# Layer 2 of a two-block model on one core: the first gate tile projected inside the query and key projections

## The chip, the core and the metric

The kernel runs on one core of one Trainium2 chip. The metric is the device time of one execution in microseconds, of which a run gives one number; lower is better. The span in the profile is the time from the first to the last instruction of the program on the core, and is a little shorter than the device time. TensorE's clock has two levels here, 2.4 GHz (written 1.00 in the rows) and 1.2 GHz (0.50).

## What is computed

Two blocks of two layers each work on 512 tokens of 1024 features in float32. The first block has a mixer of dilated windows (layer 1) and a differential attention (layer 2); the second has twice a hybrid mixer and a feed-forward part. Only layer 2 is touched. Its core is this:

```
def diff_mixer(h, w_in, lq1, lk1, lq2, lk2, subln, w_out, lambda_init):
    proj = h @ w_in
    q = proj[..., :DIFF_QK_WIDTH]
    k = proj[..., DIFF_QK_WIDTH:2 * DIFF_QK_WIDTH]
    v = proj[..., 2 * DIFF_QK_WIDTH:2 * DIFF_QK_WIDTH + DIFF_WIDTH]
    gate = proj[..., 2 * DIFF_QK_WIDTH + DIFF_WIDTH:]
    ...
    p = jax.nn.softmax(s, axis=-1)
    a = p[:, 0] - lam * p[:, 1]
    ...
    o = rmsnorm(o, subln) * (1.0 - lambda_init)
    y = o.reshape(B, S, DIFF_WIDTH) * jax.nn.silu(gate)
    return y @ w_out
```

There are 8 heads of 128 value columns; each head has two softmaxes over causal scores.

## The kernel before

**One list of steps, five queues.** The class `Order` writes one list of steps for the whole program, and each engine (TensorE, VectorE, ScalarE, GpSimd, and SyncE for the DMAs) then walks that list and issues its own part of each step. So the list is also the order on every engine, and an engine waits in place for whatever its next instruction needs. Every product of float32 is made as three: weights and activations are held as a high part and a rest, and high times high, high times rest and rest times high are added up.

**Weights.** `weight_tiles` lists the weight tiles in the order in which they are used. A tile is split into its two parts when its turn comes (step `split`, the high part by ScalarE at L2161 or L2165; steps `lo`, the rest by GpSimd at L3151 or L3153), into one of three places that are used in turn.

**Main and side.** In layer 2 (`layer2`) a main generator issues projections in pieces: `wide` for the values (tiles l2v0 and l2v1, L1789), `rotated` for queries and keys (l2q0 to l2q3 and l2k0 to l2k3, pieces of 12 matmuls at L1782; each tile is followed by its rotary step on VectorE, L2527: `rope` reads the banks, `rotate` combines, and the DMAs of `spread` lay the result out), and `gates` for the gate tiles (l2g0 to l2g3, pieces of 12 matmuls of 256 columns, L1789). `beside` lets the side generator, the attention, advance by a fixed ratio for each piece: R_L2 = 1.2 beside the projections and R_G2 = 1.35 beside the gates.

**Attention.** There are 32 units, 8 for each pair of heads (p = 0 to 3); a unit is one head and one block of 128 queries, with 128 to 512 keys. The blocks of the eight units of a pair have 128, 384, 256, 256, 128, 384, 512 and 512 keys, in this order (`L2_ORDER`). A unit n goes through five stages, of which several units are in flight: `scores2` (TensorE L1955 into banks 4 and 5; then VectorE masks and reduces, L2774), `exp2` (ScalarE L2321), `mix2` (VectorE L2786 to L2791), `turn2` (TensorE transposes the weights, L1966; ScalarE copies them, L2346), `out2` (TensorE L1977; ScalarE squares and scales the sums, L2335 and L2337). Scores need both banks 4 and 5, so the next scores wait for VectorE to have reduced the ones before. The transposes, the sums and the transposes of the gated output (`chunk`, TensorE L1855, ScalarE L2206, VectorE L2573) share two corner banks, 6 and 7, which are taken in turn: each user waits until the last but one has been read out.

**Waits of the main generator.** The queries of pair 2 are held back until the attention of pair 0 is through (`while p >= 2 and p - 2 not in attended`), and gate tile j until pair j is normalized (`done(j)`; `square2` on VectorE, a power on GpSimd at L3168, `norm2` on VectorE). While the main generator is held back, only attention steps are issued, and TensorE has no projection to do between them. A gate tile j is projected, `gate` makes gate times (1 + tanh) in `fat(3072..)` (ScalarE L2291, VectorE L2686), `times` multiplies the normalized output by it (VectorE L2700), and `chunk` transposes it for the output projection.

## Time and profile before

| | us |
|---|---|
| Median of 3 runs | 2664.75 (2664.47 to 2665.68) |
| The profiled execution, device time | 2664.24 |
| The profiled execution, span | 2662.9 |
| TensorE busy with matmuls | 2616.2 (98%) |
| VectorE busy | 1227.3 (46%) |
| ScalarE busy | 1039.0 (39%) |
| GpSimd busy | 1141.6 (43%) |

The busy times are averages over stages that differ. Matmuls overlap, and their recorded ends are modelled; where a stretch is costed closely, the distance from one start to the next is the better measure. An idle time is printed behind the row of the instruction that it precedes, with what ended it.

### The profile page before, as it was taken

To read this page: it belongs to the slowest core of one execution; us is meant where nothing else is said; L and a number is where in the kernel's file an instruction comes from. 1 tells how busy PE (TensorE), PEld (TensorE's weight loads), DVE (VectorE), ACT (ScalarE), POOL (GpSimd) and SP (SyncE) were. 2 spreads that over 40 slices of the span, in tenths; PEclk is the share of its full clock that TensorE was granted. 3 is DMA by queue.
4 is the path that set the end of the run, shared out by engine and by line. 5 is a ranking of instruction groups with operands and counts; after the bars stand their busy time and mean duration, and the time that the engine had idled before them with its cause. 6 is when DMAs were issued, how large, how long until landed. Compare 5 with 4: busy or idle time off the path is not lost.

```text
span 2662.9 us, 35461 instructions
## 1 busy us (share of the span) xinstructions
PE 2616.2 (98%) x13561; PEld 2122.7 (80%) x13561; DVE 1227.3 (46%) x2446; ACT 1039.0 (39%) x1937; POOL 1141.6 (43%) x894
## 2 busy tenths in 40 slices
PE   8999999989999999999999999999999999999998
PEld 6887878768778877777888888887777788888887
DVE  3535344543565456445245424265544524642426
ACT  4343434443446344452333424234435333342422
POOL 4434434435442443333464444444333336544443
PEclk9999999999999999999999999999999999999999
DMA  6434333332331332224352333324222435233331
GB/s 195 129 105 120 103 110 112 112 111 85 114 92 60 110 102 80 80 83 143 107 175 80 111 95 99 99 77 136 86 73 91 135 107 183 72 118 95 95 95 64
DMA packets 215053, 282.15 MB, mean 106 GB/s; under 512 B 21982, under 2 KB 155586, under 8 KB 214116
## 3 DMA queue, kind: packets, MB, share of 16 engines
q1 hardware_dynamic: 214884, 279.88, 34.1%
q8 instruction: 108, 1.77, 0.3%
q14 instruction: 61, 0.50, 0.1%
HBM read 246.21 MB, written 16.84 MB: 99 GB/s over the span
## 4 chain that ended last, share of the span: by engine, by line
PE 93%; DVE 3%; ACT 2%; POOL 1%; issue 1%; DMA 0%; DVEq 0%; ACTq 0%; POOLq 0%
PE banks L1789 36%; PE banks L1786 31%; PE banks L1782 13%; PE banks L1807 2%; PE banks L1921 1%; PE banks L1903 1%; PE banks L1846 1%; PE banks L1955 1%; PE banks L2022 1%; PE banks L2049 1%; PE banks L1977 1%; PE banks L1889 1%; PE banks L2035 1%; DVE AR L2527 1%; PE banks L2100 1%
## 5 line engine op out<-in xcount | busy, mean ns | idle before, releaser
L3153 POOL TENSOR_TENSOR WS<-WR,WS 128x512 fp32r<-128x512 f32 (+2 forms) x676 | 856.9, 1301 | 1030.1 <-ACT WS L2165 1030.1
L1789 PE MATMUL banks<-WS,UT 128*128 128x512 f32 (+1 forms) x3312 | 720.6, 370 | 4.8 <-DVE UT L2527 4.8
L1786 PE MATMUL banks<-UT,WS 128*128 128x512 f32 (+1 forms) x3024 | 705.1, 392 | 0.7 <-ACT AR L2354 0.7
L1786 PEld LDWEIGHTS banks<-UT,WS 128*128 128x128 f32 (+1 forms) x3024 | 561.8, 187 | 129.3 <-issue 12.0
L1789 PEld LDWEIGHTS banks<-WS,UT 128*128 128x128 f32 x3312 | 559.8, 188 | 116.2 <-issue 18.1
L2165 ACT ACTIVATE WS<-WR 128x1024 fp32r<-128x1024 f32 (+1 forms) x344 | 333.2, 1018 | 215.7 <-PE banks L1789 139.0
L1782 PE MATMUL banks<-UT,WS 128*128 128x512 f32 x1536 | 365.8, 394 | 0.0
L1782 PEld LDWEIGHTS banks<-UT,WS 128*128 128x128 f32 x1536 | 283.9, 188 | 63.7 <-issue 5.9
L1789 PE MATMUL banks<-WS,AT 128*128 128x512 f32 x1296 | 300.7, 390 | 3.8 <-POOL WS L3153 3.3
L1789 PEld LDWEIGHTS banks<-WS,AT 128*128 128x128 f32 x1296 | 242.7, 188 | 55.1 <-POOL WS L3153 3.7
L3151 POOL TENSOR_TENSOR WS<-WR,WS 128x512 fp32r<-128x512 f32 x128 | 179.6, 1434 | 231.1 <-ACT WS L2161 231.1
L2527 DVE TENSOR_TENSOR AF<-banks,AF 128x512 f32<-128x512 f32 x128 | 94.0, 786 | 188.9 <-PE banks L1782 188.7
L3088 DVE SCALAR_TENSOR_TENSOR AR<-banks,AR 128x511 f32<-128x511 f32 x84 | 63.0, 750 | 211.7 <-ACT AR L2496 211.7
L3168 POOL TENSOR_TENSOR SM<-SM 128x1 f32<-128x1 f32 (+2 forms) x44 | 47.4, 1076 | 238.0 <-DVE SM L3056 90.9
L2527 DVE TENSOR_TENSOR AR<-AR,banks 128x512 f32<-128x512 f32 x80 | 57.4, 724 | 169.2 <-PE banks L1789 157.5
L2527 DVE TENSOR_TENSOR AR<-AR 128x512 f32<-128x512 f32 (+3 forms) x93 | 93.3, 1003 | 16.3 <-ACT AR L2246 12.9
L2496 ACT ACTIVATE AR<-banks,AR 128x512 f32<-128x512 f32 x84 | 65.1, 774 | 89.4 <-PE banks L1786 79.7
L2161 ACT ACTIVATE WS<-WR 128x512 fp32r<-128x512 f32 x128 | 69.9, 622 | 57.4 <-PE banks L1782 57.4
L2629 DVE CUSTOM_DVE_ANT_0 AF<-banks,MF 128x256 f32<-128x256 f32 (+1 forms) x128 | 44.4, 402 | 101.7 <-PE banks L1889 86.4
L2527 DVE TENSOR_TENSOR AF<-AF 128x512 f32<-128x512 f32 x64 | 88.7, 1424 | 0.7
L1786 PE MATMUL banks<-AT,WS 128*128 128x512 f32 x384 | 87.4, 389 | 0.0
L1786 PEld LDWEIGHTS banks<-AT,WS 128*128 128x128 f32 x384 | 72.1, 188 | 15.0
(224 smaller groups left out, 2517.0 us busy)
## 6 DMA issues: line engine op xcount, KB each, us to landing
WR<-in_w_in SPq DMA_DIRECT2D x112, 512.0 KB, 3.6
WR<-in_w_up SPq DMA_DIRECT2D x88, 512.0 KB, 3.5
WR<-in_dil_w_in SPq DMA_DIRECT2D x64, 512.0 KB, 3.7
WR<-in_w_down SPq DMA_DIRECT2D x40, 512.0 KB, 3.7
WR<-in_diff_w_in SPq DMA_DIRECT2D x32, 512.0 KB, 3.8
WR<-in_dil_w_in SPq DMA_DIRECT2D x32, 256.0 KB, 3.7
AR<-AF SPq DMA_DIRECT2D x128, 64.0 KB, 2.7
AR<-AF SPq DMA_DIRECT2D x64, 128.0 KB, 2.6
```

Of the source, the lines that this page charges most:

```text
L1782: mm = pe.matmul(B[bank][:, :], slot(i, part)[:, c:c + P], act[:, other, kk, :], start=start, stop=stop)
L1786: mm = pe.matmul(B[bank][0:c, :], w[part][:, kk, g * P:g * P + c], act[:, other, kk, :], start=start, stop=stop)
L1789: mm = pe.matmul(B[bank][:, off:off + n], act[:, other, before_k + kk, g * P:g * P + P], w[part][:, kk, :], start=start, stop=stop)
L1807: mm = pe.matmul(B[c][:, 256 * half:256 * half + 256], w[x][:, kk, (c % 2) * P:(c % 2) * P + P], UT[:, y, kk, 256 * half:256 * half + 256] ...
L2161: x = se.activation(slot(i, 0)[:, to].rearrange("p (a f c) -> p a f c", f=2, c=32), src, ACT.Copy)
L2165: se.activation(slot(i, 0)[:, v * h:v * h + h], raw(i)[:, v * h:v * h + h], ACT.Copy).then_inc(hi.sem, 1)
L2496: se.activation(d, B[order.bank[i, half][0]][:, :], ACT.Identity, scale=cp[:, 2, f:f + 1], bias=cp[:, 3, f:f + 1]).then_inc(conv_id.sem, 1)
L2527: return ve.tensor_tensor(out_, x, y, op)
L3088: ve.scalar_tensor_tensor(d[:, 1:T], bank[:, 0:T - 1], cp[:, 1, f:f + 1], d[:, 1:T], ALU.mult, ALU.add).then_inc(dve_step, 1)
L3151: ge.tensor_tensor(low, src, high.bitcast(F32), ALU.subtract).then_inc(lo_p.sem, 1)
L3153: ge.tensor_tensor(slot(i, 1)[:, s], raw(i)[:, s], slot(i, 0)[:, s].bitcast(F32), ALU.subtract).then_inc(lo_p.sem, 1)
L3168: ge.tensor_tensor(SM[:, o:o + n], SM[:, o:o + n], SM[:, MHALF:MHALF + n], ALU.pow).then_inc(rstd.sem, 1)
```

## The change

The first gate tile, l2g0, moves in the list of tiles and in the list of steps: it is projected right after the second tile of values, ahead of the queries of pair 2. Its `gate` step (ScalarE and VectorE) goes with it. Its `times` steps stay with the gates: `gates` now begins with them, once pair 0 is normalized, and then goes on with tile l2g1. The last hunk of the diff keeps a wait pointing at the gate tile before, now that it is not the neighbour in the list.

```
--- before.py
+++ after.py
@@ -118,9 +118,11 @@
     for p in range(4):
         if p % 2 == 0:
             wide(f"l2v{p // 2}", w, 2048 + 256 * p)
+        if p == 2:
+            out.append(("l2g0", KC, 256, [(0, cols(w, 3072))]))
         for name, o in (("q", 0), ("k", 1024)):
             out.append((f"l2{name}{p}", KC, 256, [(0, cols(w, o + 256 * p))]))
-    for j in range(4):
+    for j in range(1, 4):
         out.append((f"l2g{j}", KC, 256, [(0, cols(w, 3072 + 256 * j))]))
     joined("l2o", ap["diff_w_out"][0])
     for l in range(2):
@@ -519,9 +521,15 @@
             self.hybrid(l)
             self.ffn(l)
 
-    def gates(self, name, done, late, gated):
+    def gates(self, name, done, late, gated, early=()):
+        for i, half, j in early:
+            while not done(j):
+                self.tick()
+                yield 1
+            self.step("times", i, half, j)
+            self.soon(4 + 2 * half, lambda half=half: self.step("chunk", name, half))
         across = self.feature_major if name == "l1g" else self.token_major
-        for j in range(4):
+        for j in range(1 if early else 0, 4):
             while j < 3 and not done(j):
                 self.tick()
                 yield 1
@@ -646,11 +654,16 @@
         self.step("natural_table")
 
     def layer2(self):
-        projected, attended, normed = set(), set(), set()
+        projected, attended, normed, early = set(), set(), set(), []
 
         def project(p):
             if p % 2 == 0:
                 yield from self.wide(f"l2v{p // 2}", self.plain("copy", "2v", p), fresh=(p == 0))
+            if p == 2:
+                def deal(i, half):
+                    self.step("gate", i, half, 0)
+                    early.append((i, half, 0))
+                yield from self.token_major("l2g0", deal)
             while p >= 2 and p - 2 not in attended:
                 yield 1
             for name in "qk":
@@ -701,7 +714,7 @@
         late = []
         att = attention()
         self.beside(main(), att, R_L2)
-        self.beside(self.gates("l2g", lambda j: j in normed, late, set()), att, R_G2)
+        self.beside(self.gates("l2g", lambda j: j in normed, late, set(), early), att, R_G2)
         self.lower(self.splits)
         self.drain(att)
         self.flush()
@@ -2287,7 +2300,7 @@
                     i, half, j = a
                     se.wait_ge(proj.sem, proj.at[i, half if tiles[i][0][:3] == "l1g" else 2 * half + 1])
                     if j > 0:
-                        se.wait_ge(timed.sem, timed.at[i - 1, half])
+                        se.wait_ge(timed.sem, timed.at[index[f"{tiles[i][0][:3]}{j - 1}"], half])
                     se.activation(fat(3072 + 512 * half, 512), B[gate_bank(i, half)][:, :], ACT.Tanh,
                                   scale=0.5).then_inc(tanhed.sem, 1)
```

No instruction is added or removed but the grouping; what changes is the place of each. In the rows below a name before `<-` is what is written, those behind it what is read; WS holds split weights, UT the layer's input, CT the identity, AF, AR and MF are work space. Rows of the attention's scores (L1955) and sums (L1977) have twice the count in the trace; projections and transposes stand one for one. Line numbers from L1782 on are 13 higher in the changed kernel.

**TensorE, from the last piece of l2g1 to the first piece of l2g2, before:**

```order
L1789 MATMUL banks<-WS,UT 128x256 x12
L1966 MATMUL banks<-CT,MF 128x128 x4
L1955 MATMUL banks<-AR 128x256 x4
L1977 MATMUL banks<-AR,AF 128x128 x4
L1966 MATMUL banks<-CT,AF 128x128
L1855 MATMUL banks<-CT,AR 128x128 x4
L1977 MATMUL banks<-AR,AF 128x128
L1966 MATMUL banks<-CT,AF 128x128 x3
L1855 MATMUL banks<-CT,AR 128x128 x4
L1955 MATMUL banks<-AR 128x128 x2
L1955 MATMUL banks<-AR 128x384 x2
L1789 MATMUL banks<-WS,UT 128x256 x12
```

**The same place now,** the first 12 rows from the last piece of l2g1 on:

```order
L1802 MATMUL banks<-WS,UT 128x256 x12
L1968 MATMUL banks<-AR 128x512 x2
L1990 MATMUL banks<-AR,AF 128x128 x2
L1979 MATMUL banks<-CT,MF 128x128
L1968 MATMUL banks<-AR 128x512 x2
L1868 MATMUL banks<-CT,AR 128x128 x4
L1990 MATMUL banks<-AR,AF 128x128
L1979 MATMUL banks<-CT,AF 128x128 x3
L1968 MATMUL banks<-AR 128x128 x2
L1968 MATMUL banks<-AR 128x384 x2
L1868 MATMUL banks<-CT,AR 128x128 x4
L1990 MATMUL banks<-AR,AF 128x128 x3
```

Before, the last 12 matmuls of l2g1 stood behind the sums of unit 22, and 10 rows of attention separated them from l2g2 (the last row). Now they stand ahead of the scores of unit 22 (the first row of 512). All 11 rows shown behind them are attention and `chunk`; 10 more follow, from the transposes of unit 22 to the scores of units 28 and 29, before the first 12 matmuls of l2g2.

**VectorE, after the rotary products of the last key tile (l2k3), before:**

```order
L2786 RECIPROCAL SM<-SM 128x2
L2788 SCALAR_TENSOR_TENSOR SM<-SM 128x1
L2791 SCALAR_TENSOR_TENSOR MF<-MF,SM 128x384
L2527 TENSOR_TENSOR AF<-AF 128x512 x2
L2774 ISA AF,SM<-banks,CT 128x256
L2774 ISA SM 128x1
L2774 ISA AF,SM<-banks,CT 128x256
L2774 ISA SM 128x1
```

**The same place now:**

```order
L2799 RECIPROCAL SM<-SM 128x2
L2801 SCALAR_TENSOR_TENSOR SM<-SM 128x1
L2804 SCALAR_TENSOR_TENSOR MF<-MF,SM 128x384
L2713 SCALAR_TENSOR_TENSOR AR<-AF,AR 128x2x256 x2
L2540 TENSOR_TENSOR AF<-AF 128x512 x2
L2787 ISA AF,SM<-banks,CT 128x256
L2787 ISA SM 128x1
L2787 ISA AF,SM<-banks,CT 128x256
L2787 ISA SM 128x1
```

The two `times` instructions of l2g0 (AR<-AF,AR) now stand between the mix of unit 17 (the row MF<-MF,SM) and the rotation of l2k3 (AF<-AF 128x512 x2). The reduction of unit 19 stands behind them.

**TensorE, the end of pair 1's attention, before:**

```order
L1977 MATMUL banks<-AR,AF 128x128
L1782 MATMUL banks<-UT,WS 128x512 x12
L1966 MATMUL banks<-CT,AF 128x128 x3
L1977 MATMUL banks<-AR,AF 128x128 x3
L1966 MATMUL banks<-CT,MF 128x128 x4
L1977 MATMUL banks<-AR,AF 128x128 x4
L1782 MATMUL banks<-UT,WS 128x512 x12
L1966 MATMUL banks<-CT,AF 128x128 x4
L1977 MATMUL banks<-AR,AF 128x128 x4
L1782 MATMUL banks<-UT,WS 128x512 x60
```

**The same place now:**

```order
L1990 MATMUL banks<-AR,AF 128x128
L1979 MATMUL banks<-CT,AF 128x128 x3
L1795 MATMUL banks<-UT,WS 128x512 x12
L1990 MATMUL banks<-AR,AF 128x128 x3
L1979 MATMUL banks<-CT,MF 128x128 x4
L1990 MATMUL banks<-AR,AF 128x128 x4
L1979 MATMUL banks<-CT,AF 128x128 x4
L1990 MATMUL banks<-AR,AF 128x128 x4
L1795 MATMUL banks<-UT,WS 128x512 x96
```

Before, one piece of the key tile stood between the sums of unit 14 and the transposes of unit 15. Now units 13, 14 and 15 end in one stretch with no piece between them.

## Rows read from the trace of the kernel before

**Rows 1.** From the page: engines' busy time; the chain that ended last.

```profile
PE 2616.2 (98%) x13561; PEld 2122.7 (80%) x13561; DVE 1227.3 (46%) x2446; ACT 1039.0 (39%) x1937; POOL 1141.6 (43%) x894
...
PE 93%; DVE 3%; ACT 2%; POOL 1%; issue 1%; DMA 0%; DVEq 0%; ACTq 0%; POOLq 0%
```

**Rows 2.** Timeline of TensorE, hole before l2g2: start, us, what, [idle before it].

```profile
824.99 1.66 PE L1789 MATMUL banks<-WS,UT 128*128 128x256 f32 x12
...
832.76 0.88 PE L1966 MATMUL banks<-CT,AF 128*128 128x128 f32 x3 [1.77 <-DVE AT L2573]
...
834.42 1.79 PE L1955 MATMUL banks<-AR 64*128 64x128 f32 x8
836.14 1.63 PE L1789 MATMUL banks<-WS,UT 128*128 128x256 f32 x12
```

**Rows 3.** Windows: length, busy us (PE, PEld, DVE, ACT, POOL), granted clock, DMA.

```profile
829.00:832.40 3.40, 1.42 (x10) 0.87 (x8) 2.62 (x11) 3.12 (x12) 1.64 (x1) 1.00 0.00 0
832.40:835.80 3.40, 3.04 (x15) 2.29 (x15) 1.73 (x9) 2.08 (x7) 0.00 (x0) 0.50 0.01 2
```

**Rows 4.** Groups by form, 686 to 864 us: count, busy us, mean ns, idle before.

```profile
L2161 ACT ACTIVATE WS<-WR 128x512 fp32r<-128x512 f32 x16 | 8.7, 626 | 0.0
...
L2321 ACT ACTIVATE AF<-AF,SM 128x512 f32<-128x512 f32 x12 | 8.5, 720 | 0.0
...
L2346 ACT ACTIVATE AF<-banks 128x512 f32<-128x512 f32 x8 | 4.8, 598 | 4.7 <-PE banks L1966 4.7
...
L2206 ACT ACTIVATE AT<-banks,SM 128x512 fp32r<-128x512 f32 x4 | 2.7, 679 | 1.7 <-PE banks L1855 1.7
...
L2774 DVE CUSTOM_DVE_ANT_0 AF<-banks,CT 128x512 f32<-128x512 f32 x12 | 7.8, 687 | 8.9 <-PE banks L1955 8.9
...
L2573 DVE SCALAR_TENSOR_TENSOR AT<-banks,SM,AT 128x512 fp32r<-128x512 f32 x4 | 3.0, 751 | 4.1 <-ACT AT L2206 4.1
...
L2791 DVE SCALAR_TENSOR_TENSOR MF<-MF,SM 128x512 f32<-128x512 f32 x2 | 1.5, 751 | 0.1
```

**Rows 5.** Timeline of VectorE around the last two rotations of layer 2.

```profile
780.64 3.42 DVE L2527 TENSOR_TENSOR AF<-AF 128x512 f32<-128x512 f32 x2
...
794.37 1.29 DVE L2527 TENSOR_TENSOR AF<-AF 128x512 f32<-128x512 f32 x2
795.57 0.42 DVE L2774 CUSTOM_DVE_ANT_0 AF<-banks,CT 128x256 f32<-128x256 f32 x1
...
801.61 0.69 DVE L2700 SCALAR_TENSOR_TENSOR AR<-AF,AR 128x512 f32<-128x512 f32 x1
```

**Rows 6.** Timeline of GpSimd there (rest parts of two gate tiles).

```profile
780.51 5.98 POOL L3153 TENSOR_TENSOR WS<-WR,WS 128x512 fp32r<-128x512 f32 x4 [4.26 <-ACT WS L2165]
795.62 5.27 POOL L3153 TENSOR_TENSOR WS<-WR,WS 128x512 fp32r<-128x512 f32 x4 [9.13 <-ACT WS L2165]
```

**Rows 7.** Timeline of TensorE: scores of units 20 and 21.

```profile
797.51 1.14 PE L1955 MATMUL banks<-AR 64*128 64x128 f32 x8
798.58 1.64 PE L1789 MATMUL banks<-WS,UT 128*128 128x256 f32 x12
```

**Rows 8.** Timeline of TensorE: end of pair 1's attention.

```profile
758.58 0.49 PE L1966 MATMUL banks<-CT,AF 128*128 128x128 f32 x3
759.65 0.94 PE L1977 MATMUL banks<-AR,AF 128*128 128x128 f32 x6 [0.58 <-ACT AF L2346]
...
762.14 1.16 PE L1977 MATMUL banks<-AR,AF 128*128 128x128 f32 x8 [1.12 <-ACT AF L2346]
763.06 3.02 PE L1782 MATMUL banks<-UT,WS 128*128 128x512 f32 x12
765.91 0.60 PE L1966 MATMUL banks<-CT,AF 128*128 128x128 f32 x4
767.20 1.16 PE L1977 MATMUL banks<-AR,AF 128*128 128x128 f32 x8 [0.69 <-ACT AF L2346]
768.11 13.88 PE L1782 MATMUL banks<-UT,WS 128*128 128x512 f32 x60
```

More of the change, by code:

```diff
@@ L120, in weight_tiles @@
             wide(f"l2v{p // 2}", w, 2048 + 256 * p)
+        if p == 2:
+            out.append(("l2g0", KC, 256, [(0, cols(w, 3072))]))
         for name, o in (("q", 0), ("k", 1024)):
             out.append((f"l2{name}{p}", KC, 256, [(0, cols(w, o + 256 * p))]))
-    for j in range(4):
+    for j in range(1, 4):
         out.append((f"l2g{j}", KC, 256, [(0, cols(w, 3072 + 256 * j))]))
@@ L520, in program, with gates @@
             self.ffn(l)
-    def gates(self, name, done, late, gated):
+    def gates(self, name, done, late, gated, early=()):
+        for i, half, j in early:
+            while not done(j):
+                self.tick()
+                yield 1
+            self.step("times", i, half, j)
+            self.soon(4 + 2 * half, lambda half=half: self.step("chunk", name, half))
         across = self.feature_major if name == "l1g" else self.token_major
-        for j in range(4):
+        for j in range(1 if early else 0, 4):
             while j < 3 and not done(j):
@@ L648, in layer2 @@
     def layer2(self):
-        projected, attended, normed = set(), set(), set()
+        projected, attended, normed, early = set(), set(), set(), []
         def project(p):
@@ L653, in project, with deal @@
                 yield from self.wide(f"l2v{p // 2}", self.plain("copy", "2v", p), fresh=(p == 0))
+            if p == 2:
+                def deal(i, half):
+                    self.step("gate", i, half, 0)
+                    early.append((i, half, 0))
+                yield from self.token_major("l2g0", deal)
             while p >= 2 and p - 2 not in attended:
@@ L703, in layer2 @@
         self.beside(main(), att, R_L2)
-        self.beside(self.gates("l2g", lambda j: j in normed, late, set()), att, R_G2)
+        self.beside(self.gates("l2g", lambda j: j in normed, late, set(), early), att, R_G2)
         self.lower(self.splits)
@@ L2289, in scalar @@
                     if j > 0:
-                        se.wait_ge(timed.sem, timed.at[i - 1, half])
+                        se.wait_ge(timed.sem, timed.at[index[f"{tiles[i][0][:3]}{j - 1}"], half])
                     se.activation(fat(3072 + 512 * half, 512), B[gate_bank(i, half)][:, :], ACT.Tanh,
```

## The prediction

> **What bounds the kernel now.** The page comes first: TensorE is busy for 98% of the span, and 93% of the chain that ended last is its own work [rows 1]. The change adds no matmul and removes none, so it can only move the time by what TensorE loses between matmuls: waits in place, and stretches at the lower clock. The next view is therefore the timeline of TensorE over layer 2, read for the rows with an idle time behind them and, since recorded ends are modelled, for distances from start to start. Beside the projections there is almost none. The losses sit where the main generator is held back and attention stands alone: the end of pair 1's attention [rows 8] and the hole before l2g2 [rows 2]. The change shortens the first kind of stretch and lengthens the second, since the pieces of l2g0 that covered attention late now cover it early.
>
> **Early: projection beside units 7 to 12.** Before, the units around 7 to 9 ran with nothing between while l2q2 was held back; no idle time over 0.2 us stands there. The eight pieces of l2g0 now lie between them. I take 0.2 us gained, for the hand-offs too short to be printed, and between 0 and 0.5. The gate step of l2g0 is two instructions of the size of a `times`, 0.7 us each [rows 5], in a stretch where VectorE has time; nothing waits for them.
>
> **End of pair 1.** Before: from 758.58 to 768.11 are 9.53 us [rows 8]. One piece inside takes 765.91 - 763.06 = 2.85. The sums of a 512-key unit take 768.11 - 767.20 = 0.91 (0.11 per row of 128), so the sums of units 13 to 15 are 0.69 + 0.91 + 0.91, and their 3 + 4 + 4 transposes, at about 0.09 (an estimate, a little under a row of sums of the same width), are 1.0. 9.53 - 2.85 - 3.5 = 3.2 lost. Now units 13, 14 and 15 end without the piece between, but the same two round trips remain: transpose, ScalarE's copy of 0.60 [rows 4], sums. ScalarE has the split of l2k3 (4 instructions, 8.7 / 16 x 4 = 2.2 us [rows 4]) just ahead of unit 13's output, which puts the copy of unit 14 some 0.8 us later relative to the sums of unit 13, while one of the three waits goes under the piece ahead. I work out 3.1 lost. Change: -0.1, between -1.2 (one round trip hidden) and +1.
>
> **Unit 20's scores.** This is a new wait. The two `times` of l2g0 stand on VectorE between the mix of unit 17 and the rotation of l2k3. One takes 0.69, and 0.61 to the next start [rows 5]; two push the rotation from 794.37 to about 795.65. That matters since GpSimd starts the rest part of the next gate tile at 795.62 and works on it until 800.9 [rows 6]. The rotation of l2q3 ran beside GpSimd's same work (780.51 to 786.49) and took 3.42 instead of 1.29 [rows 5, 6]. So the rotation of l2k3 is now likely to take 3.35 to the next start: it ends at 799.0. Behind it stands the reduction of unit 19 (two of 0.42, until 799.8), and the scores of units 20 and 21 wait for the banks it frees. Before, they started at 797.51, a slack of over 1 us behind the reduction (795.57) [rows 5, 7]. Loss: 799.8 - 797.5 = 2.3 us. Bounds: 0, should the rotation stay ahead of GpSimd and take 1.29 (reduction over at 797.7, just beside the scores), and 3, should GpSimd slow the second `times` too.
> The Trainium skill (GPSIMD Engine Reference, section Specifications) says that GpSimd shares its SBUF interfaces with VectorE and that VectorE instructions with two SBUF inputs contend with it. The rotation is one of these. By a reading without that rule this term would be 0.2 and the sum 2 us smaller; the trace agrees with the rule (3.42 against 1.29).
>
> **The hole before l2g2.** Before, from the end of the last piece of l2g1 at 824.99 + 1.66 = 826.65 to the start of l2g2 at 836.14 are 9.5 us [rows 2]. Part of it is the clock: TensorE was busy for 1.42 of 3.40 us, then ran at half the clock for 3.4 us [rows 3]. In that stretch the rows from 832.76 to 836.14 took 3.4 us for three transposes, four chunk transposes and a pair of scores that take 0.25 + 0.44 + 1.07 = 1.8 at the full clock (1.07 is 798.58 - 797.51 [rows 7]): 1.6 lost.
> Now the hole begins at the scores of unit 22. The attention moved into it is: scores of unit 22, of unit 23, and of 24 and 25, 3 x 1.07; sums of units 19 to 22, 20 recorded rows at 0.11; transposes of 20 to 22, 8 at 0.09: 6.1 us. This is no loss, it only stood elsewhere. The length of the new hole has to be walked along its waits. With 0 at the end of the last piece:
> VectorE does gate (0.7 to 1.4) and `times` (to 2.0), then the reduction of unit 22, two of 0.69 [rows 4], to 3.3. Scores of 512 keys fill both banks, so those of unit 23 wait for that: 3.4 to 4.5. Reduction of 23: to 5.8. Transposes of `chunk` 2: 4.4 to 5.0; ScalarE 0.68, until 5.75; VectorE 0.75 behind the reduction, until 6.55 [rows 4]. The corner bank of unit 21's transposes waits for exactly this, as the 1.77 us wait did before [rows 2]: 6.7 to 7.0. Scores of 24 and 25 to 8.1, `chunk` 3 to 8.6. ScalarE has the two exponentials of unit 23 in front (2 x 0.72, until 9.0 [rows 4]), then its part of the chunk to 9.6, VectorE's to 10.4. Unit 22: transposes 10.5 to 11.0, copy 0.60 to 11.7, sums 11.8 to 12.9. Unit 23: transposes, and scores of 26 and 27 to 14.3, sums to 15.4. ScalarE squares, VectorE's `square2` waits for that, the mix of unit 25 behind it ends at 17.1, the reduction of unit 27 at 17.8, and the scores of 28 and 29 run from 17.9 to 19.0. For a handful of hand-offs that I took at 0.05 each I add 0.2: **19.2 us**.
> 19.2 - 9.5 - 6.1 = **+3.6 us**, at full clock throughout. Bounds: +1.9, if the hand-offs overlap better by one chunk round trip (0.68 + 0.75 + latency), and +6.8, if the clock falls twice for 1.6 each.
>
> **What stays.** From l2g2 on the order is unchanged, and the DMAs are no term: the weights of each tile are still fetched two tiles ahead, and l2g0 takes a turn in the places as any tile. The `spread` DMAs of l2k3 leave some 2 us later and are needed 20 us later, for unit 24.
>
> **Sum.** -0.2 - 0.1 + 2.3 + 3.6 = +5.6 us on the profiled execution of 2664.24: 2669.8. The median of the runs is 0.5 above it, so I predict **2670.3**. A measurement of this kernel can tell about 0.2%, 5.3 us, from no change; the bound of slower is then 2670.1, and the forecast stands barely beyond it.
>
> **Rivals.**
> The clock falls again in the new hole. It has waits of about 1.8 and 1.6 us and five shorter ones; before, the fall followed a stretch with 1.42 of 3.40 us busy [rows 3]. In my walk TensorE is busy for half of the hole, and no part is as empty, so I leave the fall out of the forecast. One fall costs up to 1.6: 2671.9. The Trainium skill (TensorE: Matmul & The Clock Gate, section HAM oscillation) warns that bursts separated by waits start cold again and again; by that rule this rival is the case, perhaps twice, and the time 2672 to 2673.5. The trace holds against it that the waits at the end of pair 1 (1.12 and 0.69 us) left the clock up [rows 8].
> The rotation stays ahead of GpSimd, or costs only the `times`: the 2.3 shrinks to about 0.2, time 2668.2, no measurable change. For it speaks that the margin between 795.65 and 795.62 is nothing; against it, that even a rotation starting 0.5 us before GpSimd has its second half inside.
> The hole is shorter than walked: VectorE and ScalarE enter it with less queued and the chunks' round trips overlap. At +1.5 for the hole: 2668.2; with the rival above, 2666.
> Faster: the early cover pays and the late hole costs nothing. Its place is the hole, its mechanism that attention already ran at its own pace beside l2g1, so that pair 2 is normalized at the same moment whether pieces stand between or not. Then the fall of the clock (1.6) and the round trip at pair 1 (1.2) would be gains: 2664.75 - 3 = 2661.7. It decides from a hole of less than 9.5 + 6.1 - 2.3 = 13.3 us. Against it: the walk gives 19.2, and its links are waits that the rows name already (VectorE's read-out of the chunk, 1.77 [rows 2]).
> That the change does not do what it says is excluded by the order.
>
> **Chances.** Forecast, 0.45, within 1 us of 2670.3, half of it a little above; clock falls, 0.15; rotation unharmed, 0.15; shorter hole, 0.2; faster, 0.05. Above 2670.1 lie about 0.35 of the forecast's 0.45, all of the clock's, and little of the others (0.02): 0.52 slower. Faster by over 0.2% (under 2659.4): 0.02. Within: 0.46. The range is from 2666.4 (shorter hole with an unharmed rotation) to 2673.0 (clock falls with a longer hole); outside are the faster case and the double fall with all bounds.
>
> **What would show it.** The profile after should have a start of unit 20's scores some 2 us later behind the piece before, with an idle time put down to VectorE; the rotation of l2k3 at over 3 us instead of 1.29; a hole of about 19 us between the last piece of l2g1 and l2g2 with waits of over 1 us before the scores of unit 23 and the transposes of unit 21; and no half clock there. From l2g2 on, every distance should be as before. The prediction is wrong if the hole is under 16 us or over 22, or if the scores of unit 20 start without a wait.

## The result and the profile after

| | before | after |
|---|---|---|
| Median of 14 runs each, on the same chip, us | 2665.21 (2663.9 to 2666.2) | 2670.52 (2669.63 to 2673.17) |
| Ratio, with its 95% interval | | 1.0023 (1.0014 to 1.0031) |
| The profiled execution, device time, us | 2664.24 | 2673.17 |

The change made the kernel slower by 5.3 us, against a forecast of 5.6 us over the profiled execution of before and a predicted 2670.3. The 14 runs of after lie in two groups, though: nine from 2669.6 to 2671.0 (median 2669.91) and five from 2672.6 to 2673.2 (median 2673.09), and the five have a granted clock of 0.996 as their mean, the others 0.996 to 0.998. The profiled execution is the highest of the upper group. Three executions far outside all others are left out of what follows: the profiled one of e6_cover_first (3747.98, granted clock 0.65) and two of the kernel before that ran beside the experiments (5288.75 and 2920.11).

In the changed kernel every line below the diff's last hunks stands 13 lower than in [rows 2 to 8]: scores L1968, transposes L1979, sums L1990, chunk L1868, pieces L1795 and L1802. TensorE is as busy as before, and the chain is as much its own, so the page shows nothing of the cause (busy times of the engines; chain by engine):

```profile
PE 2620.8 (98%) x13561; PEld 2125.4 (80%) x13561; DVE 1231.7 (46%) x2446; ACT 1039.3 (39%) x1937; POOL 1144.6 (43%) x894
...
PE 92%; DVE 3%; ACT 2%; POOL 1%; issue 1%; DMA 0%; SPq 0%; DVEq 0%; ACTq 0%; POOLq 0%
```

The timeline of TensorE does. First the end of pair 1's attention, which answers to [rows 8] (start, us, what, [idle before it]):

```profile
762.74 0.49 PE L1979 MATMUL banks<-CT,AF 128*128 128x128 f32 x3
...
765.84 0.83 PE L1990 MATMUL banks<-AR,AF 128*128 128x128 f32 x6
...
768.67 1.16 PE L1990 MATMUL banks<-AR,AF 128*128 128x128 f32 x8 [1.56 <-ACT AF L2359]
...
771.12 1.16 PE L1990 MATMUL banks<-AR,AF 128*128 128x128 f32 x8 [0.86 <-ACT AF L2359]
772.03 3.24 PE L1795 MATMUL banks<-UT,WS 128*128 128x512 f32 x13
```

1.56 + 0.86 = 2.42 us of printed waits stand against 0.58 + 1.12 + 0.69 = 2.39 before. Two waits hold what three held. By the distance of starts, from the transposes of unit 13 to the piece behind unit 15, the same work takes 772.03 - 762.74 = 9.29 us against 9.53 before. Next the scores of unit 20, the transposes beside l2g1, and the hole, with what answers to [rows 2, 7] (same columns):

```profile
810.80 1.14 PE L1968 MATMUL banks<-AR 64*128 64x128 f32 x8 [1.13 <-DVE SM L2787]
...
816.91 0.41 PE L1979 MATMUL banks<-CT,AF 128*128 128x128 f32 x2 [0.91 <-DVE AT L2586]
...
820.96 1.63 PE L1802 MATMUL banks<-WS,UT 128*128 128x256 f32 x12
...
826.14 1.58 PE L1968 MATMUL banks<-AR 64*128 64x512 f32 x4 [1.74 <-DVE SM L2787]
...
830.42 0.87 PE L1979 MATMUL banks<-CT,AF 128*128 128x128 f32 x3 [1.23 <-DVE AT L2586]
...
836.01 1.06 PE L1979 MATMUL banks<-CT,AF 128*128 128x128 f32 x4 [0.38 <-DVE AT L2586]
837.76 1.16 PE L1990 MATMUL banks<-AR,AF 128*128 128x128 f32 x8 [0.69 <-ACT AF L2359]
...
843.93 1.14 PE L1968 MATMUL banks<-AR 64*128 64x128 f32 x8
845.00 1.65 PE L1802 MATMUL banks<-WS,UT 128*128 128x256 f32 x12
```

The hole goes from 820.96 + 1.63 = 822.59 to 845.00: 22.4 us. The two waits of over a microsecond that were announced are there: before the scores of unit 23 (826.14) and the transposes of unit 21 (830.42). What was not announced is the clock. In the hole, by windows (length, busy us of PE, PEld, DVE, ACT, POOL, granted clock):

```profile
822.60:826.70 4.10, 2.36 (x13) 1.10 (x13) 3.15 (x9) 2.28 (x8) 0.00 (x0) 1.00 0.00 0
823.30:826.70 3.40, 1.66 (x11) 0.88 (x9) 3.15 (x9) 1.58 (x6) 0.00 (x0) 1.00 0.00 0
826.70:836.90 10.20, 8.60 (x35) 5.50 (x31) 5.70 (x17) 5.53 (x17) 0.00 (x0) 0.50 0.00 0
836.90:845.00 8.10, 6.14 (x44) 4.22 (x43) 5.46 (x24) 7.21 (x28) 1.64 (x1) 1.00 0.01 3
```

TensorE was busy for 2.36 of 4.10 us, and in the last 3.40 of them for 1.66. Then it ran at half its clock for 10.2 us, three times as long as before [rows 3].

To set kernels beside each other without what happens elsewhere in the program, I take the start of the row of layer 2's first scores (unit 0), that of its last scores (unit 31), and the distance between. The hole is from the end of the last piece of l2g1 to the start of the first of l2g2. The last column tells the length of the stretches at half clock in the hole; the windows put their ends to about 0.2 us.

| Kernel | first scores | last scores | distance | against before | hole | half clock |
|---|---|---|---|---|---|---|
| before | 686.74 | 849.67 | 162.9 | | 9.5 | 3.4 |
| after | 687.91 | 858.58 | 170.7 | +7.7 | 22.4 | 10.2 |
| e1_extra | 687.54 | 861.61 | 174.1 | +11.1 | 9.7 | 3.4 |
| e2_times_later | 687.51 | 856.53 | 169.0 | +6.1 | 22.6 | 3.4 + 3.4 |
| e3_cover | 686.05 | 854.95 | 168.9 | +6.0 | 20.7 | none |
| e4_dense | 688.05 | 859.42 | 171.4 | +8.4 | 19.6 | 3.4 + 2.3 |
| e5_before_cover | 686.41 | 848.91 | 162.5 | -0.4 | 9.0 | none |
| e7_cover_first_times_later | 687.55 | 853.39 | 165.8 | +2.9 | 19.7 | none |
| e8_chunks_later | 687.46 | 858.26 | 170.8 | +7.9 | 20.4 | 10.2 |
| e9_before_chunks_later | 687.43 | 848.07 | 160.6 | -2.3 | 6.3 | none |
| e10_all_three | 686.31 | 850.83 | 164.5 | +1.6 | 17.5 | none |
| e11_cover_first_again | 685.99 | 853.60 | 167.6 | +4.7 | 19.5 | none |

The profiled execution of after lost 7.7 us in layer 2, and 1.2 us before it began (687.91 against 686.74), in a part that the change doesn't touch. There too the clock differed: layer 1 has a stretch at half clock of 10.2 us (581.0 to 591.2), against 3.4 before. Whether that made the 1.2 us is not shown, since the profiles of e7 and e10 have the same 10.2 us there, with first scores at 687.55 and 686.31.

### The profile page after: what moved, and what is told of

Same layout as the page of the kernel before. It is cut to its first block, busy times and chain, and to the rows that moved or that the text cites. A ratio compares the mean times of both kernels' runs of the same rounds, so it can differ in the third digit from the quotient of the medians.

```text
span 2671.9 us, 35461 instructions
## 1 busy us (share of the span) xinstructions
PE 2620.8 (98%) x13561; PEld 2125.4 (80%) x13561; DVE 1231.7 (46%) x2446; ACT 1039.3 (39%) x1937; POOL 1144.6 (43%) x894
## 3 DMA queue, kind: packets, MB, share of 16 engines
q8 instruction: 108, 1.77, 0.3%
## 4 chain that ended last, share of the span: by engine, by line
PE 92%; DVE 3%; ACT 2%; POOL 1%; issue 1%; DMA 0%; SPq 0%; DVEq 0%; ACTq 0%; POOLq 0%
PE banks L1802 35%; PE banks L1799 31%; PE banks L1795 13%; PE banks L1820 2%; PE banks L1934 1%; PE banks L1916 1%; PE banks L1859 1%; PE banks L2035 1%; PE banks L2062 1%; PE banks L1968 1%; PE banks L1902 1%; PE banks L2048 1%; DVE AR L2540 1%; PE banks L1990 1%; PE banks L2113 1%
## 5 line engine op out<-in xcount | busy, mean ns | idle before, releaser
L1802 PE MATMUL banks<-WS,UT 128*128 128x512 f32 (+1 forms) x3312 | 720.1, 370 | 4.7 <-DVE UT L2540 4.7
L1802 PEld LDWEIGHTS banks<-WS,UT 128*128 128x128 f32 x3312 | 559.7, 188 | 113.9 <-issue 15.8
L1795 PE MATMUL banks<-UT,WS 128*128 128x512 f32 x1536 | 365.0, 393 | 0.0
L1795 PEld LDWEIGHTS banks<-UT,WS 128*128 128x128 f32 x1536 | 284.1, 188 | 64.6 <-issue 6.7
L1802 PE MATMUL banks<-WS,AT 128*128 128x512 f32 x1296 | 301.8, 391 | 2.5 <-POOL WS L3166 2.0
L1802 PEld LDWEIGHTS banks<-WS,AT 128*128 128x128 f32 x1296 | 243.4, 189 | 54.4 <-POOL WS L3166 2.7
```

The lines of the kernel that those rows point to most:

```text
L1795: mm = pe.matmul(B[bank][:, :], slot(i, part)[:, c:c + P], act[:, other, kk, :], start=start, stop=stop)
L1802: mm = pe.matmul(B[bank][:, off:off + n], act[:, other, before_k + kk, g * P:g * P + P], w[part][:, kk, :], start=start, stop=stop)
```

## The experiments

**Early half alone.** The kernel before with one gate tile more, projected where the change projects l2g0, and used by nothing; the four gate tiles stay where they were.

```
         if p % 2 == 0:
             wide(f"l2v{p // 2}", w, 2048 + 256 * p)
+        if p == 2:
+            out.append(("l2gx", KC, 256, [(0, cols(w, 3072))]))
...
+            if p == 2:
+                yield from self.token_major("l2gx", lambda i, half: None)
             while p >= 2 and p - 2 not in attended:
```

> The kernel before with one more gate tile projected early, where the change puts l2g0; its result is thrown away (no gate, no multiplication), and all else, l2g0 at its old place too, stays. It tells the early half of the change from the late half. Theory (all the loss is late, the early cover gains a little): the extra tile costs its 96 matmuls, 8 pieces at 1.46 us = 11.7 us, less the 0.8 us by which units 7 to 15 lose less between matmuls: 2665.2 + 11.7 - 0.8 = 2676.1, with the hole before l2g2 at about 9.5 us as before and the scores of unit 20 without a wait. Rival (the early tile itself disturbs the attention, through the splits moved on ScalarE and GpSimd): 2678 or more, and waits over 1 us before l2q3 that before does not have.

Measured: 2674.32 (2672.99 to 2676.33, 5 runs), 9.6 us over the 2664.68 of before, and 1.8 under what I expected. The eight pieces take 8 x 1.46 = 11.7 us by the distance of their starts. In its profile the scores of unit 16 stand 10.88 us later than before relative to the first scores; so the early half gains 0.8 us by its profile, which is the slowest of the five runs; by the medians it gains 11.7 - 9.6 = 2.1. The end of pair 1 has the same two waits of 1.56 and 0.86 and the same length of 9.29 us as in after, against 9.53 before. So 0.24 of the 0.8 us are gained there and some 0.5 ahead of it, in the hand-offs around units 7 to 13. And its hole is as before (timeline of TensorE; transposes are L1970 here):

```profile
836.66 1.66 PE L1793 MATMUL banks<-WS,UT 128*128 128x256 f32 x12
...
844.44 0.87 PE L1970 MATMUL banks<-CT,AF 128*128 128x128 f32 x3 [1.78 <-DVE AT L2577]
...
847.99 1.68 PE L1793 MATMUL banks<-WS,UT 128*128 128x256 f32 x12
```

The wait of 1.77 us from [rows 2] is here as 1.78, and the scores of unit 20 start without a wait. The loss of the change comes from the late half alone.

**The two multiplications behind the rotation.** The changed kernel, with the `times` of l2g0 and the chunks that follow them a few steps later.

```
-            self.step("times", i, half, j)
-            self.soon(4 + 2 * half, lambda half=half: self.step("chunk", name, half))
+            self.soon(2 + half, lambda i=i, half=half, j=j: self.step("times", i, half, j))
+            self.soon(5 + 2 * half, lambda half=half: self.step("chunk", name, half))
```

> The changed kernel with the two multiplications of l2g0 issued 2 and 3 ticks into l2g1, behind the rotation of l2k3, and chunks 0 and 1 one tick later. Theory (the multiplications push the rotation under GpSimd's work, and unit 20's scores wait for it): the rotation takes 1.3 us again instead of 2.4, the 1.13 us wait before the scores of unit 20 goes, and the time falls by about 1.2 us against the changed kernel, to 2669.3 (2668.5 where the clock stays up, 2672 where it falls for long). Rival (VectorE is only slower by GpSimd's own start, whatever stands before): rotation 2.4 us or more, no change of time.

Measured: 2668.86 (2666.64 to 2671.17, 11 runs), 1.7 us under the median of after; the ratio to before is 1.0017 (1.0008 to 1.0026). In after, VectorE and GpSimd stood like this (timelines):

```profile
806.46 1.29 DVE L2713 SCALAR_TENSOR_TENSOR AR<-AF,AR 128x512 f32<-128x512 f32 x2
807.67 2.40 DVE L2540 TENSOR_TENSOR AF<-AF 128x512 f32<-128x512 f32 x2
809.98 0.41 DVE L2787 CUSTOM_DVE_ANT_0 AF<-banks,CT 128x256 f32<-128x256 f32 x1
...
811.24 1.48 DVE L2804 SCALAR_TENSOR_TENSOR AF<-AF,SM 128x256 f32<-128x256 f32 x1
...
817.12 0.48 DVE L2804 SCALAR_TENSOR_TENSOR AF<-AF,SM 128x256 f32<-128x256 f32 x1
```

```profile
807.72 6.17 POOL L3166 TENSOR_TENSOR WS<-WR,WS 128x512 fp32r<-128x512 f32 x4 [9.13 <-ACT WS L2178]
```

With the multiplications later (VectorE, then GpSimd):

```profile
806.05 1.28 DVE L2540 TENSOR_TENSOR AF<-AF 128x512 f32<-128x512 f32 x2
807.25 0.42 DVE L2787 CUSTOM_DVE_ANT_0 AF<-banks,CT 128x256 f32<-128x256 f32 x1
...
807.94 2.90 DVE L2713 SCALAR_TENSOR_TENSOR AR<-AF,AR 128x512 f32<-128x512 f32 x2
```

```profile
807.30 5.96 POOL L3166 TENSOR_TENSOR WS<-WR,WS 128x512 fp32r<-128x512 f32 x4 [9.13 <-ACT WS L2178]
```

The rotation takes 1.28 us ahead of GpSimd's work and 2.40 where GpSimd starts 0.05 us behind it; the two multiplications take 1.29 alone and 2.90 inside; a mix step of one size takes 0.48 and 1.48. The reductions, which read a bank, take 0.41 and 0.42 either way. With the order turned round, the scores of unit 20 start without a wait, and the 0.91 us before the transposes at 816.91 are down to 0.20, one step on, before the sums (timeline of TensorE):

```profile
809.19 1.14 PE L1968 MATMUL banks<-AR 64*128 64x128 f32 x8
...
816.18 0.68 PE L1990 MATMUL banks<-AR,AF 128*128 128x128 f32 x4 [0.20 <-DVE AT L2586]
```

So this one edit removes two waits, one announced and one not. A little comes back: the first wait in the hole is 1.99 us instead of 1.74.

**Filler in the hole.** The changed kernel, with three matmuls of 256 columns behind each of the 13 steps in the hole; they write a bank that the next piece overwrites.

```
             while j < 3 and not done(j):
                 self.tick()
+                if j == 2:
+                    self.step("cover")
...
+                    for kk in range(3):
+                        pe.matmul(B[order.bank[i, 0][0]][:, 0:256], UT[:, 0, kk, 0:P], weight(i, 0)[:, kk, :],
+                                  start=True, stop=True)
```

> The changed kernel with filler in the hole before l2g2: at each of the ticks in which the gates wait for pair 2, TensorE gets 3 more matmuls of 256 columns (weights of l2g2, into l2g2's bank, overwritten afterwards), some 14 x 3 x 0.122 = 5 us of work that nothing needs. Theory (the loss in the hole is waiting for VectorE and ScalarE, plus the half clock that follows from it, and the spread of the runs from 2669.6 to 2673.2 is the clock): the filler lies mostly in the waits and keeps the clock at 1.00 over the whole hole; the hole is 19 to 22 us, the time 2669 to 2671, and the runs lie within 1 us of each other. Rival (the spread has another cause, and the hole is bound by TensorE's own work): the time rises by the filler's 5 us to 2675, with the same spread.

Measured: 2669.79 (2669.24 to 2671.19, 11 runs), ratio 1.0022 (1.0013 to 1.0031). The upper group of runs is gone, and no half clock stands in the hole, which is 1.8 us shorter with 39 matmuls more in it. The median is only 0.1 us under the 2669.91 of after's lower group. They are not free: from the sums of unit 22 to the scores of unit 28 the start distance is 7.39 us against 6.17 in after (843.93 - 837.76).

**Denser attention beside l2g1.** The changed kernel, with the ratio at 2.1 instead of 1.35 while l2g1 is projected, so that less is left for the hole.

```
-            acc += ratio * t
+            acc += (ratio() if callable(ratio) else ratio) * t
...
-        self.beside(self.gates("l2g", lambda j: j in normed, late, set(), early), att, R_G2)
+        self.beside(self.gates("l2g", lambda j: j in normed, late, set(), early), att, lambda: 2.1 if self.tiles[self.opened - 1][0] in ("l2g1",) else R_G2)
```

> The changed kernel with attention advancing by 2.1 steps instead of 1.35 beside the pieces of l2g1 alone, so that two units more stand beside them and two fewer in the hole. Theory (the hole loses because attention stands alone there, by about 1 us a unit with the clock): the hole shrinks from 22 to some 15 us, of which 3.5 us is work that moved out; the time falls by 1.5 to 4 us against the changed kernel, to 2667 to 2669. Rival (VectorE and ScalarE are the bound of the whole stretch, so waits appear beside l2g1 instead): the time stays at 2670 to 2671 and waits of over 1 us stand between the pieces of l2g1.

Measured: 2675.68 (2672.17 to 2676.3, 5 runs), ratio 1.0039 (1.0026 to 1.0051): 5 us slower than after by the medians, where I had expected it faster. Three of the five runs are at 2675.7 to 2676.3 and two at 2672.2 and 2672.9; upper with upper and lower with lower, it is some 3 us slower. The hole is 2.8 us shorter, but TensorE now waits beside l2g1, and longer in what is left of the hole (timeline of TensorE, then one row of VectorE):

```profile
809.87 1.14 PE L1968 MATMUL banks<-AR 64*128 64x128 f32 x8 [1.44 <-DVE SM L2787]
...
823.47 0.30 PE L1979 MATMUL banks<-CT,MF 128*128 128x128 f32 x1 [1.21 <-DVE AT L2586]
...
841.10 0.33 PE L1979 MATMUL banks<-CT,AF 128*128 128x128 f32 x1 [1.46 <-DVE AF L2804]
...
844.36 0.52 PE L1979 MATMUL banks<-CT,AF 128*128 128x128 f32 x3 [2.02 <-DVE AT L2586]
```

```profile
839.51 0.75 DVE L2586 SCALAR_TENSOR_TENSOR AT<-banks,SM,AT 128x512 fp32r<-128x512 f32 x1 [3.88 <-ACT AT L2219]
```

In the table the distance of this kernel is only 0.7 us over that of after, but it holds one piece less: ten pieces of 12 matmuls stand behind the last scores instead of nine, and from there to the first `chunk` behind the projections are 881.88 - 859.42 = 22.5 us instead of 20.2. So attention doesn't get through sooner by being issued sooner; its round trips only wait elsewhere. They go through ScalarE as well as VectorE: the wait at 841.10 is put down to VectorE, but VectorE itself had stood idle for 3.88 us for ScalarE's part of a chunk. My expectation counted the shorter hole and not the waits in front of it.

**Filler in the hole of before.** The edit of e3_cover in the kernel before (15 matmuls).

> The kernel before, with three matmuls of 256 columns of l2g2's first piece put behind each step of attention in its own hole (15 in all, some 1.8 us of TensorE; the piece that follows overwrites them, so nothing of the result depends on them). Theory (the fall of the clock is a price by itself, and the waits leave room for the filler): no half clock between 825 and 840, 1.6 us less, some 0.3 us for filler that finds no wait: 2663.4, between 2662.9 and 2664.2. Rival (the links of the hole are those of VectorE and ScalarE at any clock, and the filler only pushes them): 2664.7 to 2665.5.

Measured: 2664.26 (2663.51 to 2665.36, 11 runs) beside 2664.66, ratio 0.9999 (0.9990 to 1.0008): between the two expectations, and no change of time by that interval. The clock stays up:

```profile
826.30:835.30 9.00, 7.25 (x58) 5.72 (x56) 6.01 (x21) 7.14 (x24) 1.64 (x1) 1.00 0.00 1
```

The hole is only 0.5 us shorter. The transposes of unit 25 stand 833.02 - 826.32 = 6.7 us into it, against 832.76 - 826.65 = 6.1 before; from there to l2g2 are 2.3 us, with 0.5 of filler, against 3.4. So the price of 1.6 for the half clock holds (3.4 - 2.3 + 0.5), and the filler takes back 1.1 of it.

**Filler behind the first seven steps only**, in the changed kernel.

```
+        covers = 7
...
+                if j == 2 and name == "l2g" and covers:
+                    covers -= 1
+                    self.step("cover")
```

> The changed kernel with the filler of the covered run, but only behind the first seven steps in the hole (up to the transposes of unit 22), none behind the six after them. In the covered run the stretch from the sums of unit 22 to the scores of unit 28 took 7.39 us against 6.17 without filler, so the theory takes those 1.2 us off: a hole of 19.4 us (19.2 walked blind), no half clock in it, 2668.6. Rival (the clock only stayed up because the filler ran to the end of the hole): a half clock from about 835 on, hole 21 to 22 us, 2669.8 to 2670.8.

Measured: 2669.51 (2668.61 to 2670.12, 10 runs), ratio 1.0019 (1.0009 to 1.0028), between the two expectations. Since its profiled execution is the one left out, the same kernel was run again.

> The same kernel as the one with filler behind the first seven steps only, for a profile of it: expected there is a hole of 19.4 to 19.9 us at the full clock, with waits before the scores of unit 23 and the transposes of 21 and 22, and 2669.5 again. Rival: a half clock from about 835 on in part of the executions.

Measured: 2669.14 (2668.07 to 2670.06, 8 runs), ratio 1.0018 (1.0008 to 1.0028). This is the nearest to the changed kernel's hole at the full clock; 21 matmuls of filler are in it (timeline of TensorE, then windows):

```profile
818.89 1.63 PE L1806 MATMUL banks<-WS,UT 128*128 128x256 f32 x12
...
824.08 1.13 PE L1981 MATMUL banks<-AR 64*128 64x512 f32 x4 [1.03 <-DVE SM L2800]
...
827.46 0.52 PE L1992 MATMUL banks<-CT,AF 128*128 128x128 f32 x3 [0.73 <-DVE AT L2599]
...
831.41 0.63 PE L1992 MATMUL banks<-CT,AF 128*128 128x128 f32 x4 [0.40 <-DVE AT L2599]
...
838.90 1.14 PE L1981 MATMUL banks<-AR 64*128 64x128 f32 x8
839.97 1.68 PE L1806 MATMUL banks<-WS,UT 128*128 128x256 f32 x12
```

```profile
820.50:828.00 7.50, 5.74 (x37) 3.68 (x36) 6.19 (x17) 4.56 (x15) 0.00 (x0) 1.00 0.01 2
828.00:840.00 12.00, 9.99 (x74) 7.32 (x74) 8.05 (x32) 10.43 (x37) 1.64 (x1) 1.00 0.00 1
```

From 820.52 to 839.97 are 19.45 us, against the 19.2 that were walked, and against 22.4 in after. In front of the scores of unit 23 the filler costs nothing: they stand 3.56 us into the hole, and 3.55 in after, where the clock fell only behind them. Behind each later filler TensorE still has a printed wait, but what the filler costs there isn't measured, so 19.45 may be a little too long. By it the half clock of 10.2 us cost 3.0 us, and the two groups of after lie 3.2 apart. The median gained less, 1.0 to 1.4; that only some executions of after had such a fall is what the groups suggest, as no execution of the lower group was profiled.

**Both.** Filler behind the first seven steps, and the multiplications behind the rotation.

> The same with the two multiplications of l2g0 behind the rotation of l2k3. If the causes add up, the two waits beside l2g1 (1.2 us before the scores of unit 20 and 0.75 before transposes of unit 18) go as in the run with the later multiplications (1.66 us in the median): 2668.6 - 1.7 = 2666.9. Rival (the later multiplications and chunks only shift VectorE's work into the hole, whose links then lengthen by the same): 2668 to 2668.8.

Measured: 2667.95 (2666.9 to 2669.02, 11 runs), ratio 1.0012 (1.0003 to 1.0021). In layer 2 it is +2.9 us against +4.7 with the filler alone, so the multiplications are worth 1.8 us by the profiles and 1.2 to 1.6 by the medians. The total is 1 us above what I expected, as the kernel with the filler alone was by 0.5 to 0.9.

**Chunks out of the hole.** The changed kernel with chunk 2 and 3 beside l2g2.

```
-                        self.soon(4, lambda: self.step("chunk", name, 2 * j))
-                        self.soon(6, lambda: self.step("chunk", name, 2 * j + 1))
+                        n = 16 if name == "l2g" and j == 1 else 4
+                        self.soon(n, lambda: self.step("chunk", name, 2 * j))
+                        self.soon(n + 4, lambda: self.step("chunk", name, 2 * j + 1))
```

> The changed kernel with the last two of l2g1's transposes of the gated values (chunk 2 and 3) taken out of the hole and put beside l2g2. Theory of the walk (the corner bank of the transposes of units 21 and 22 waits for VectorE's read-out of these chunks, and VectorE's 0.75 and ScalarE's 0.68 us of each chunk lie on the chain): the waits before the transposes of units 21 and 22 go, the hole is 2.5 to 4 us shorter of which 0.9 us of TensorE's work only moves, and beside l2g2 come back two waits of some 0.75: time 2668 to 2669.5. Rival (the exponentials and reductions set the pace, the chunks fit in beside them): the hole shrinks by no more than the 0.9 us of work, 2670.5 to 2671.5.

Measured: 2669.56 (2667.93 to 2673.45, 9 runs), ratio 1.0021 (1.0012 to 1.0031), 1 us under after. Three of the nine runs are at 2672.9 to 2673.5, where after's upper group is, and the distance in layer 2 is no shorter (+7.9 against +7.7), so a gain is not shown. The waits before the transposes of units 21 and 22 are gone, but a shorter one stands before the scores of 24 and 25, and a new one beside l2g2, where ScalarE has a chunk in front of the copy for unit 26 (timeline of TensorE):

```profile
828.33 2.08 PE L1969 MATMUL banks<-AR 64*128 64x128 f32 x8 [0.47 <-DVE SM L2788]
...
849.64 0.71 PE L1991 MATMUL banks<-AR,AF 128*128 128x128 f32 x4 [1.35 <-ACT AF L2360]
```

The hole is 2.0 us shorter, all of which comes back beside l2g2, and the clock fell in it for 10.2 us in this profile as well. So the corner bank is one link of the hole, and a place ahead of transposes isn't the place for a chunk. The edit has a side effect in this run and the next two: the same lines serve layer 1, where chunks 1 and 3 now stand two steps later. The first scores of layer 2 (687.46, 687.43 and 686.31) lie within the range of the other kernels.

**The same in the kernel before**, at places where sums come next (first wait 7 instead of 16).

> The kernel before, with chunk 2 and 3 taken out of its hole and put beside l2g2, each at a place where the next step is a set of sums and not transposes (chunk 1 comes one step later beside l2g1). Theory (VectorE's read-out of a chunk holds the corner bank that the next transposes want): the wait of 1.77 us before the transposes of unit 25 goes, these stand at about 831.2 instead of 832.76, l2g2 starts at about 833.1 instead of 836.14, 0.9 us of transposes come back beside l2g2: 2 us less, 2662.9 (2662 to 2663.5), the lowest time of all. Rival (the hole is paced by exponentials and reductions, or the chunks bring their waits along to where they now stand, as ScalarE's did at 849.64 in the run with later chunks in the changed kernel): 2664.2 to 2665.5.

Measured: 2662.75 (2661.17 to 2666.16, 11 runs) beside 2664.29, ratio 0.9996 (0.9987 to 1.0005): the lowest time of all kernels here, though its gain can't be told from none by that interval. The profile has what was expected (timeline of TensorE):

```profile
825.66 1.64 PE L1790 MATMUL banks<-WS,UT 128*128 128x256 f32 x12
...
830.86 0.49 PE L1978 MATMUL banks<-AR,AF 128*128 128x128 f32 x2 [0.38 <-ACT AF L2347]
831.89 0.55 PE L1967 MATMUL banks<-CT,AF 128*128 128x128 f32 x3 [0.55 <-DVE AF L2792]
832.58 1.14 PE L1956 MATMUL banks<-AR 64*128 64x128 f32 x8
833.65 1.64 PE L1790 MATMUL banks<-WS,UT 128*128 128x256 f32 x12
```

In place of the 1.77 us wait for the chunk's read-out [rows 2] are 0.55 us for the mix of the unit itself, the hole is 6.3 us instead of 9.5, no half clock is in it, and layer 2 is 2.3 us shorter. This run doesn't part the shorter wait (1.2 us) from the half clock that is gone with it (1.6 by the filler run), so not all of the 2.3 us is the bank's.

**All three** in the changed kernel (filler behind seven steps, multiplications later, chunk 2 and 3 beside l2g2 where sums come next).

> The changed kernel with all three: filler behind the first seven steps of the hole, the two multiplications of l2g0 behind the rotation of l2k3, and chunk 2 and 3 beside l2g2 where sums come next. If the three causes found so far are all there is besides the hole's own length, the 2667.95 of the run with the first two falls by some 1.7 us: 2666.2 (2665.5 to 2667), still 1.5 us or more above the kernel before, since the attention without projections beside it stays longer than it was. Rival (the links that remain take up what the chunks free): 2667.5 to 2668.3.

Measured: 2666.33 (2665.45 to 2672.95, 11 runs), ratio 1.0011 (1.0002 to 1.0020). Ten runs are at 2665.5 to 2667.0; the one at 2672.95 has a granted clock of 0.948, which no other of the runs that are kept has. The causes add up as expected, and a hole of 17.5 us remains.

## Why the prediction was right, and where its steps were off

**By its own signs** the prediction is half right. Seen were the wait of unit 20's scores, the two waits over a microsecond in the hole, and unchanged distances from l2g2 on. Not seen were a rotation of over 3 us (2.40), scores of unit 20 some 2 us later (1.2), and a hole at the full clock. The hole of the profiled execution, 22.4 us, is over the 22 that I had named as the bound of being wrong, and its 2673.17 is just outside the range; the median is inside.

**The hole** was the largest term, and its working holds at the full clock: 19.2 us walked, 19.45 measured with filler in it. It holds link by link: the scores of unit 23 stand at 3.6 us into the hole (walked 3.4), the transposes of unit 21 at 6.9 (6.7), those of unit 22 at 10.9 (10.5), the scores of unit 28 at 18.4 (17.9). One link answered to its own edit, the read-out of the chunk. VectorE's reduction ahead of unit 23's scores is named by the traces (1.74 us in after, 1.03 with filler), but no run took it away. The net is 19.45 - 9.5 = 9.95 less the moved work of 6.1: +3.85, against +3.6. In the 9.5 of before, its own half clock of 1.6 is left in, as in the prediction.

**The clock** is the step that failed in the profiled execution. I left the fall out, as the working had TensorE busy for half of the hole "and no part is as empty" as the 1.42 of 3.40 us before, and priced a fall at up to 1.6. But my own walk had a stretch nearly as empty, ahead of unit 23's scores: 1.66 of 3.40 us in the trace. The clock fell at 826.7, behind it, stayed down for 10.2 us and cost 3.0 (22.4 - 19.45). So the rival "the clock falls again" was the case in the profiled execution, and at twice its price. Over the runs it seems to be in part: five of 14 lie 3 us above the others, and the filler, with which no half clock stands in the hole, takes this upper group away. The fall in layer 1 doesn't make the group: e7's profile has 10.2 us of it and lies on that kernel's median. The Trainium skill (TensorE: Matmul & The Clock Gate, section HAM oscillation) tells of a kernel whose bursts of matmuls start cold after each wait for a DMA. Its waits are longer than the 1.74 us here; the traces agree with its tendency for the profiled executions of after and of e8_chunks_later (10.2 us each) and e2_times_later (twice 3.4 us). I should have given this rival more than 0.15, and the fall more than one unit of length, since work at half the clock in a chain of waits delays the next link too; that this makes the 3.0 us is argued.

**Unit 20's scores** did wait, for VectorE's reduction as named, and the mechanism is shown by turning the order round. The size was off: at 810.80 with 1.13 us idle, some 1.2 us and not 2.3. The term that was mis-sized is the rotation under GpSimd: 2.40 us, not 3.42 as for l2q3. It started at 807.67, 0.05 us before GpSimd, where l2q3's had started 0.13 after it, and the first of its two combinations took 0.68 us and the second 1.79, against 1.74 and 1.76 for l2q3. In e4_dense the second, too, started just ahead of GpSimd (rotation from 807.84, GpSimd from 808.48), and both took 0.69. So a combination that starts even 0.05 us ahead ran free, and my argument that a rotation 0.5 us ahead has its second half inside did not hold there. The Trainium skill (GPSIMD Engine Reference, section Specifications) has contention for instructions with two SBUF inputs, and the traces agree: the rotation, the multiplications and the mix are slower inside GpSimd's stretch, and the reductions that read a bank are not.

**A wait that I didn't have.** The transposes at 816.91 waited 0.91 us, where the earlier chunk 0 holds the corner bank; 0.75 more than the like wait before (0.16). I had walked the corner bank through the hole but not through the pieces ahead of it, where the change also moves a chunk past transposes.

**Early cover** was worth 0.8 us with the end of pair 1, instead of 0.2 + 0.1. The end of pair 1 gained 0.24 (9.29 us against 9.53), so the hand-offs ahead of it, without a printed wait, gained some 0.5: they were under-sized at 0.2, with a bound of 0.5.

**The sum.** At the full clock the terms measured are -0.8, +1.2, +0.75 and +3.85, 5.0 us; the distance in layer 2 says 4.7, and the rest of 0.3 is within what "6.1 us of moved work" was estimated to. The forecast was 5.6. Then the fall of the clock adds 3 us in some executions. That the median of 2670.52 lies 0.2 us from the forecast is in part luck: two errors go against each other, 0.9 us too much for the waits, and nothing for the clock. The median of the lower group alone is 2669.91, 4.7 us over before. From l2g2 on nothing changed, as predicted: l2g2 starts 845.00 - 836.14 = 8.86 us later and the last scores 858.58 - 849.67 = 8.91.

What stays open is why the clock falls for 10.2 us in some executions and, as the two groups suggest, not in others: nothing in the program differs between them.

## What to carry to other kernels

Work that a held-back main stream could do is cover for a side stream whose links go through other engines; before taking it away, walk the hole it leaves link by link, which gave its length here to 0.3 us at the full clock. Beside the length, price the clock: this hole cost 3 us more when the clock fell behind a stretch with TensorE busy for 1.66 of 3.40 us, and a few filler matmuls at the waits took that away. And look at where read-outs of shared banks stand in the order: moving two transposes of the gated output out of the hole took 2.3 us from layer 2 of the kernel before, half clock included (1.5 us by the medians, which its interval can't tell from none), while issuing the side stream more densely only moved the waits and cost some 3 us.

## What the runs showed of the hardware

- Inside GpSimd's splits (four instructions of 128x512, about 6 us) VectorE's operations with two SBUF sources took two to three times as long: rotations 3.42 against 1.29 us a pair (2.40 where the first of the pair started 0.05 us ahead of GpSimd and ran free), multiplications 2.90 against 1.29, a mix 1.48 against 0.48. Reductions out of a bank took 0.41 in both. GpSimd was slowed less: 6.17 and 5.96 against 5.27 [rows 6], where VectorE had fewer such operations beside it.
- The granted clock fell to half for 10.2 us in one stretch of the hole, behind TensorE waits of 1.74 us at most; before, it had been 3.4 us. With the same program, execution times lay in two groups 3 us apart; that the fall makes the two groups is an inference from the runs with filler.
- Fifteen extra matmuls behind waits cost 1.1 us of the 1.6 that the full clock gave back: filler on an engine that waits was cheap, not free. The transposes of unit 25 came 0.6 us later behind it (6.7 against 6.1 us into the hole).
